# When the second weight tile and x rows 4 to 7 are loaded, and where three small steps of the up stage stand

## The chip, the cores and the metric

The kernel runs on one core of one Trainium2 chip. The core has five engines with instruction streams of their own: TensorE (PE: matmuls, and transposes as matmuls against an identity), VectorE (DVE), ScalarE (ACT), GpSimd (POOL) and SyncE (SP, which here only starts DMAs). They meet only at semaphores. The metric is the device time of one execution in microseconds (us), as the median of several runs.

## The reference, cut to what matters

One decoder layer on x of 1024 tokens by 1024 channels, float32:

```
p = x @ w_in                    # all mixer projections, 128 columns per weight tile
y = four attention branches on p, gated by sigmoid(x @ w_gate + b_gate), summed, @ w_out
x = layer_norm(2**0.25 * x + y)
a = x @ w_up                    # 1024 -> 2816; a = causal conv of width 3 over tokens
h = gelu(a) * (x @ w_ffn_gate)
out = layer_norm(2**0.25 * x + h @ w_down)
```

The change touches the very start (x and the first two weight tiles of w_in) and the beginning of the up stage (x @ w_up, x @ w_ffn_gate, conv, gelu).

## The kernel before

**High and low parts.** A float32 matrix is split into a rounded high part and the rest, the low part, and a product is three matmuls (hi·hi, hi·lo, lo·hi). ACT writes every high part, DVE or POOL subtracts it to make the low part. So an operand is ready only after two engines have worked one behind the other.

**The opening (step "x").** x has eight rows of 128 tokens, 512 KB each. ACT's queue starts the loads of rows 0 to 3 and then of the second weight tile (number 1, 512 KB in pieces of 512 bytes). SP's queue starts weight tile 0 (in two DMAs, of 96 and of 32 columns, the second with pieces of 128 bytes) and right behind it, waiting for nothing, rows 4 to 7. PE turns (transposes) each row in two halves, so there are 16 halves n = 0 to 15. For each half ACT writes the high part into act_hi (line 1354), then DVE the low part into act_lo (line 2142). After half 7 PE waits for all eight low parts and starts the first projection (line 737) over the tokens of rows 0 to 3. Its 24 matmuls come in four parts of six; in front of the third and the fourth stands half 8, half 9. In front of the fifth part, the first of the second projection, stands half 10. That fifth part waits for the high and the low part of weight tile 1 together (`weights`, `low=True`). Further parts follow, with the halves up to 15 among them, and then a wait for all 16 low parts.

ACT also makes the high part of the weight tiles (line 1326, `split_weights`), at fixed places of its stream: tile 0 behind half 5, tile 1 behind half 7. POOL makes the low part (line 1751) once the high part is there. Behind half 3 ACT starts two small DMAs (forget bias, sinks).

**The up stage.** Each block of 128 hidden columns (n = 0 to 21) needs seven products of half-size matrices (a Strassen-like scheme), named p = 1 to 7. The table PRODUCTS sets their order: (0,1) (1,1) (0,2) (1,2), then (0,6) (0,5) (0,7) (0,3) (0,4), (1,6) (1,5) (1,7) (1,3) (1,4), and from n = 2 (n,1) (n,6) (n,2) (n,5) (n,7) (n,3) (n,4). Products 6, 5, 7, 3 use weight sums which DVE makes in `weight_sums` (w_sum, line 2184). ACT copies the operand (op_hi, line 1371), POOL subtracts (op_lo, line 1761), PE multiplies (line 1092, twelve matmuls), and DVE adds what PE left to other products (`combine`, line 2184: up_s, gate_s). PE waits for such a sum before (n,7) (the sum of (n,6)), before (n,3) (the sum of (n,5)) and before (n,4) (the sum of (n,7)), because the product is accumulated on a bank that the sum reads. `weight_sums(q + 7)` stands behind every combine, so the sums run seven products ahead. The sums of the tokens' parts have low parts too, called t_lo 13 to 16 for the last of four token groups, on POOL (line 1833); product (0,6) needs 13, (0,5) 14, (0,7) 15 and (0,4) 16. Behind (n,4) DVE adds two taps of the convolution (line 2513). `operand_sums` are the sums for the later down stage (dn_sums), two of them behind (1,5) and two behind (1,7).

Of the kernel before, what the change touches and what calls it, by code (L numbers as in the profile page):

```python
# [254 lines left out]
AT = {np_: q for q, np_ in enumerate(PRODUCTS)}  # L255
OP_SLOTS = 8
OP_EARLY = 4
OP_AHEAD = 6
# [31 lines left out]
def build_layer(nc, x, w_in, b_forget, sinks, w_branch, w_gate, b_gate, w_out, ln1_g, ln1_b,  # L290
                w_up, w_ffn_gate, conv_w, conv_b, w_down, ln2_g, ln2_b, out):
    STEPS = steps()
# [8 lines left out]
    with ctx:  # L301
# [4 lines left out]
        w_raw = sb("w_raw", [P, 2, 1024])  # L306
# [82 lines left out]
        x_loaded = [sem(f"x_loaded{t}") for t in range(NTOK)]  # L389
# [5 lines left out]
        raw_loaded = [sem(f"raw_loaded{k}") for k in range(2)]  # L395
# [152 lines left out]
        def ring_sources(step):  # L548


            kind = step[0]
            win = w_in[0]
            if kind == "iq":
                return [(w_tile(win, IQ + P * step[1], P), NKT, P, None)]
            if kind == "ik_f_iw":

                return [((w_tile(win, IK, 96), w_tile(win, IN_WIDTH - 32, 32)), NKT, P, None)]
            if kind == "kv_c":
                return [(w_tile(win, CK, P), NKT, P, None)]
            if kind in ("q", "k", "v"):  # L560
                col = {"q": Q_COL, "k": K_COL, "v": V_COL}[kind][step[1]]
                return [(w_tile(win, col + P * step[2], P), NKT, P, None)]
            if kind == "attn" and step[2] < PAIRS - 1:
                br, pr = step[1], step[2] + 1
                return [src for k in (("k", "q", "v") if br in (B, D) else ("q",)) for src in ring_sources((k, br, pr))]
            if kind == "merge":
                br, res = step[1], []
                for dt in range(NKT + 1):
                    if dt < NKT:
                        res.append((w_tile(w_gate[0], br * D_MODEL + dt * P, P), NKT, P, None))  # L570
                    if br == FINAL and 4 <= dt < NKT:
                        res.append(wo_source(dt - 4))
                    if dt >= 1:
                        res.append((w_tile(w_branch[0, br], (dt - 1) * P, P, 4), 4, P, None))
                return res
            if kind == "outproj":
                return [wo_source(k) for k in range(4, NKT)]
            return []

        def ring_view(buf, g, kt, cols):  # L580
            return buf[:, g % 2, 0:kt * cols].rearrange("p (k c) -> p k c", c=cols)
# [550 lines left out]
        def _(sp):  # L1132
            ring = Tally()
# [73 lines left out]
                sp.dma_start(h_slot(n), src).then_inc(h_loaded[n % H_SLOTS], 16)  # L1207

            load_weights(ring_sources(STEPS[1])[0])
            ring.next()  # L1210
            for t in range(4, NTOK):
                sp.dma_start(mid[:, t, :], x[0, t * P:(t + 1) * P, :]).then_inc(x_loaded[t], 16)

            def forget_bias(h):
# [7 lines left out]
            for step in STEPS[3:]:  # L1222
# [57 lines left out]
                if step[0] == "down":  # L1280
                    for n in range(NDOWN):
# [7 lines left out]
                        if n in ROWS_AT:  # L1289
                            t = ROWS_AT.index(n)  # L1290
# [20 lines left out]
        def _(act):  # L1311
            ring, chunks, obanks, pts, vparts = Tally(), Tally(), Tally(), Tally(), Tally()
# [204 lines left out]
            pt_released = released_chunks()  # L1517
            for t in range(4):
                act.dma_start(mid[:, t, :], x[0, t * P:(t + 1) * P, :]).then_inc(x_loaded[t], 16)
            dram, kt, cols, _k = ring_sources(STEPS[2])[0]  # L1520
            act.dma_start(ring_view(w_raw, 1, kt, cols), dram).then_inc(raw_loaded[1], 16)
            for step in STEPS:
                kind = step[0]
                if kind == "x":
                    for n in range(2 * NTOK):
                        t, c = n // 2, n % 2
                        act.wait_ge(x_turned, n + 1)
                        part(act_hi[:, 4 * c:4 * c + 4, t * P:(t + 1) * P],
                             x_bank(n).rearrange("p (k t) -> p k t", k=4))
                        if n == 3:  # L1530
                            act.wait_ge(forget_set, 1)
                            act.dma_start(forget[F_AT:P, :], b_forget[0].rearrange("(h a) -> h a", a=1)
                                          ).then_inc(params_loaded, 16)
                            act.dma_start(sink[:, :], sinks[0].partition_broadcast(P)).then_inc(params_loaded, 16)
                        if n in (5, 7):
                            split_weights()
                elif kind == "iq":
                    src = pair_in(1 - step[1])
# [198 lines left out]
        def _(pool):  # L1737
# [65 lines left out]
            for step in STEPS:  # L1803
                needed += len(ring_sources(step))
                if step[0] == "attn":
                    br, pr = step[1], step[2]
                    if (br, pr) == (C, 0):
                        normalise(br, 0)
                    if pr == 0:
                        normalise(br, 1)  # L1810
                    for g in range(len(chunk_stream(br)) + 2):
                        for _p, u in asked(br, pr, g):
                            if u % 2 == 1:
                                normalise(br, u // 2)
                        if splits_at(br, pr, g):
                            split_weights()
                else:
                    split_weights(min(needed + (1 if step[0] == "v" else 2), len(ring_list)) - ring.n)
                    if step[0] == "v":
                        normalise(step[1], 0)  # L1820
                    if step[0] == "x":
                        pool.wait_ge(params_loaded, 32)
                        nc.gpsimd.tensor_scalar(sink_neg[:], sink[:], -1.0, None, ALU.mult).then_inc(consts_ready, 1)
                    if step == ("osplit", D):
                        pool.wait_ge(bias_used, 2 + HEADS)
                        distances().then_inc(dist_ready, 1)
                if step[0] == "outproj":
                    for j in range(4):
                        if j == 3:
                            operands(AT[0, 5])  # L1830
                        for i, p in enumerate((6, 5, 7, 4)):
                            pool.wait_ge(t_hi, 4 * j + i + 1)
                            nc.gpsimd.tensor_tensor(token_block(p, 1, j), t_source(p, 2 * j + 1),
                                                    token_block(p, 0, j).bitcast(F32), ALU.subtract).then_inc(t_lo, 1)
                        if j >= 1:
                            operands(2 * j - 1)
                if step[0] == "up":
                    for q in range(len(PRODUCTS)):
                        operands(q)
                if step[0] == "down":  # L1840
                    for n in range(NDOWN):
                        split_down(n)

        @block.vector
        def _(dve):
# [429 lines left out]
            for step in STEPS:  # L2275
# [193 lines left out]
                elif kind == "up":  # L2469
# [11 lines left out]
                    for q in range(4, len(PRODUCTS)):  # L2481
# [24 lines left out]
                        elif p == 4:  # L2506
# [9 lines left out]
                                if back == 1:  # L2516
                                    own(ins)
                            ins.then_inc(conv_done, 1)
                        weight_sums(q + OP_AHEAD + 1)
                        for _step in range(SUM_STEPS[min(max(n - 1, 0), 1) + (n == LAST)].get(p, 0) if n else 0):  # L2520
                            next(summing)
                    split_h(4)
# [106 lines left out]
```

## Time and profile before

| what | us |
|---|---|
| median of 3 runs | 2154.56 |
| lowest, highest | 2153.33, 2155.11 |
| the profiled execution | 2150.87 |
| its span in the trace | 2149.1 |
| PE busy | 2095.7 |
| DVE busy | 1482.3 |
| ACT busy | 935.0 |
| POOL busy | 802.3 |

The span is what the trace covers; the execution's own time is 1.8 us longer. A row of the timeline has the start, the duration, the engine, the line and operation, what is written from what, and in brackets how long the engine stood idle before and who released it. Several equal instructions in a row are merged (x2), and the duration is then that of the group.

### The profile page before, as it was taken

To read this page: it belongs to the slowest core of one execution; us is meant where nothing else is said; L and a number is where in the kernel's file an instruction comes from. 1 tells how busy PE (TensorE), PEld (TensorE's weight loads), DVE (VectorE), ACT (ScalarE), POOL (GpSimd) and SP (SyncE) were. 2 spreads that over 40 slices of the span, in tenths; PEclk is the share of its full clock that TensorE was granted. 3 is DMA by queue.
4 is the path that set the end of the run, shared out by engine and by line. 5 is a ranking of instruction groups with operands and counts; after the bars stand their busy time and mean duration, and the time that the engine had idled before them with its cause. 6 is when DMAs were issued, how large, how long until landed. Compare 5 with 4: busy or idle time off the path is not lost.

```text
span 2149.1 us, 28592 instructions
## 1 busy us (share of the span) xinstructions
PE 2095.7 (98%) x10468; PEld 1750.0 (81%) x10468; DVE 1482.3 (69%) x2532; ACT 935.0 (44%) x1671; POOL 802.3 (37%) x630
## 2 busy tenths in 40 slices
PE   8999999999999999999999999999999999999998
PEld 6788888788888888888877888888788888887887
DVE  4976767866788666666756772177877777775658
ACT  4565563126731265563126662232433333344541
POOL 2133332223322223332222332324765555555741
PEclk9999999999999999999999999999999999999999
DMA  3301101120012311112120002241566665558862
GB/s 128 41 21 30 30 16 35 45 54 21 15 45 80 87 40 30 40 45 74 45 63 2 16 11 74 79 147 50 157 190 202 182 191 176 160 193 303 276 199 94
DMA packets 198621, 198.05 MB, mean 92 GB/s; under 512 B 25161, under 2 KB 157257, under 8 KB 198481
## 3 DMA queue, kind: packets, MB, share of 16 engines
q1 hardware_dynamic: 194960, 187.26, 28.6%
q10 hardware_dynamic: 3520, 8.95, 1.2%
q8 instruction: 84, 1.38, 0.3%
q14 instruction: 57, 0.46, 0.1%
HBM read 151.06 MB, written 45.12 MB: 91 GB/s over the span
## 4 chain that ended last, share of the span: by engine, by line
PE 81%; DVE 12%; issue 3%; ACT 3%; POOL 1%; DMA 1%; DVEq 0%; SPq 0%; ACTq 0%
PE pair L737 25%; PE pair L1092 13%; PE pair L753 11%; PE obank L1092 5%; PE pair L1121 4%; PE obank L850 4%; PE chunk L829 4%; PE pair L1051 3%; DVE o_top L1899 3%; PE pair L801 3%; PE chunk L1121 2%; PE pair L802 2%; PE obank L1121 2%; DVE pt_lo L2071 1%; DVE heads L2142 1%
## 5 line engine op out<-in xcount | busy, mean ns | idle before, releaser
L1751 POOL TENSOR_TENSOR w_lo<-w_raw,w_hi 128x1024 fp32r<-128x1024 f32 (+1 forms) x102 | 219.0, 2147 | 547.6 <-ACT w_hi L1326 547.3
L737 PE MATMUL pair<-act_hi,w_hi 128*128 128x512 f32 x704 | 278.4, 396 | 4.1 <-DVE act_lo L2142 3.1
L737 PE MATMUL pair<-act_lo,w_hi 128*128 128x512 f32 x704 | 274.3, 390 | 0.0
L737 PE MATMUL pair<-act_hi,w_lo 128*128 128x512 f32 x704 | 272.4, 390 | 0.0
L1326 ACT ACTIVATE w_hi<-w_raw 128x1024 fp32r<-128x1024 f32 (+1 forms) x102 | 94.0, 922 | 366.8 <-PE pair L737 347.1
L2071 DVE TENSOR_TENSOR pt_lo<-chunk,pt_hi 128x512 fp32r<-128x512 f32 (+1 forms) x272 | 173.2, 639 | 71.5 <-ACT pt_hi L1354 66.9
L1354 ACT ACTIVATE pt_hi<-chunk 128x512 fp32r<-128x512 f32 (+1 forms) x272 | 150.7, 554 | 154.9 <-PE chunk L829 153.2
L1799 POOL TENSOR_SCALAR prob<-prob,att 128x256 f32<-128x256 f32 (+4 forms) x172 | 117.6, 694 | 255.0 <-DVE att L2015 255.0
L1899 DVE TENSOR_SCALAR_CACHE_REDUCE o_top<-score,stat 128x384 uint8<-128x384 f32 (+1 forms) x186 | 164.9, 943 | 14.0 <-issue 12.9
L753 PE MATMUL pair<-act_hi,w_hi 128*128 128x512 f32 x384 | 166.6, 434 | 0.4 <-DVE heads L2020 0.3
L737 PE MATMUL pair<-heads,w_hi 128*128 128x512 f32 x512 | 158.0, 390 | 1.7 <-DVE mid L2395 1.7
L737 PEld LDWEIGHTS pair<-act_hi,w_hi 128*128 128x128 f32 x704 | 132.3, 188 | 30.9 <-DVE act_lo L2142 3.8
L737 PEld LDWEIGHTS pair<-act_hi,w_lo 128*128 128x128 f32 x704 | 132.1, 188 | 27.9
L737 PEld LDWEIGHTS pair<-act_lo,w_hi 128*128 128x128 f32 x704 | 132.4, 188 | 24.9
L850 PE MATMUL obank<-pt_hi,heads 128*128 128x256 f32 (+1 forms) x568 | 150.8, 289 | 1.7 <-DVE o_t L2079 1.2
L753 PE MATMUL pair<-act_hi,w_lo 128*128 128x512 f32 x384 | 152.4, 397 | 0.0
L753 PE MATMUL pair<-act_lo,w_hi 128*128 128x512 f32 x384 | 151.9, 396 | 0.0
L1418 ACT ACTIVATE prob<-prob,att 128x256 f32<-128x256 f32 (+4 forms) x172 | 120.6, 702 | 43.7 <-DVE att L2003 42.0
L850 PE MATMUL obank<-pt_lo,heads 128*128 128x256 f32 (+1 forms) x568 | 139.5, 282 | 0.0
L801 PE MATMUL pair<-heads 128*128 128x512 f32 (+3 forms) x352 | 120.7, 349 | 11.8 <-DVE att L2003 6.1
L829 PE MATMUL chunk<-ident,prob 128*128 128x128 f32 x660 | 112.5, 275 | 4.6 <-DVE pt_lo L2071 3.1
L850 PEld LDWEIGHTS obank<-pt_hi,heads 128*128 128x128 f32 x568 | 108.2, 190 | 8.4 <-DVE o_t L2079 2.3
(345 smaller groups left out, 5091.1 us busy)
## 6 DMA issues: line engine op xcount, KB each, us to landing
down_sums<-dn_sums SPq DMA_DIRECT2D x40, 512.0 KB, 6.3
w_raw<-in_w_in SPq DMA_DIRECT2D x36, 512.0 KB, 3.8
w_raw<-in_w_gate SPq DMA_DIRECT2D x32, 512.0 KB, 4.0
up_raw<-in_w_up SPq DMA_DIRECT2D x22, 512.0 KB, 4.8
gate_raw<-in_w_ffn_gate SPq DMA_DIRECT2D x22, 512.0 KB, 6.0
hidden<-gelu_s SPq DMA_DIRECT2D x22, 512.0 KB, 3.3
dn_raw<-down_sums SPq DMA_DIRECT2D x44, 256.0 KB, 4.3
h_in<-down_sums SPq DMA_DIRECT2D x44, 256.0 KB, 4.7
```

The lines of the kernel that those rows point to most:

```text
L737: last = nc.tensor.matmul(dst[0:cols, s:s + HALF], w[:, k, :], a[:, k, s:s + HALF], start=(i == 0), stop=(i == len(order) - 1))
L753: last = nc.tensor.matmul(pair[1][:, s:s + HALF], w[:, k, :], a[:, k, s:s + HALF], start=(k == 0 and n == 0), stop=(k == NKT - 1 and n == 2))
L801: nc.tensor.matmul(dst[:, s:s + m], q, k_hi[:, s:s + m], start=True, stop=False)
L829: last = nc.tensor.transpose(t[:, at:at + P], prob_slot(br, 2 * j + w)[:, s:s + P], ident[:])
L850: last = nc.tensor.matmul(obank[BANK_OF[j] % 2][:, q0:q0 + width], v, part[:, slot, at:at + width], start=(c == 0 and b == 0 and w == 0), ...
L1092: last = nc.tensor.matmul(dst, w[:, cols], moving, start=(p in (1, 6, 5) and k == 0 and m == 0), stop=(k == 3 and m == 2), skip_group_chec ...
L1121: last = nc.tensor.matmul(banks[t], l[:, t * P:(t + 1) * P], r, start=(p in (6, 1, 5, 3) and k == 0 and m == 0), stop=(k == KFF - 1 and m ...
L1354: nc.scalar.activation(dst, src, func, **kw).then_inc(act_part, 1)
L1418: last = nc.scalar.activation(prob_slot(br, u)[:, 0:n], prob_slot(br, u)[:, 0:n], ACT.Exp, bias=att_stat(0, u), scale=-1.0, accum_out=att_ ...
L1751: nc.gpsimd.tensor_tensor(split_into(1, g), w_raw[:, g % 2, 0:kt * cols], split_into(0, g).bitcast(F32), ALU.subtract).then_inc(lo_ready, 1)
L1899: nc.vector.tensor_scalar(junk[:, b % 2, 0:(i + 1) * P], s, limit if isinstance(limit, float) else limit[:, b:b + 1], None, ALU.is_ge, ALU ...
L2071: nc.vector.tensor_tensor(pt_lo[:, n % PT_SLOTS, 0:m], t[:, 0:m], pt_hi[:, n % PT_SLOTS, 0:m].bitcast(F32), ALU.subtract).then_inc(chunk_f ...
```

## The change

It makes five moves and adds or removes no arithmetic.

1. The load of weight tile 1 goes from ACT's queue to SP's, between rows 5 and 6.
2. On SP, rows 4 and 5 wait until row 1 has landed; tile 1, rows 6 and 7 until row 3 has landed.
3. On ACT, the split of weight tile 1 goes from behind half 7 to behind half 9, and the two small DMAs from behind half 3 to behind half 13.
4. On POOL, the low part of the operand of (0,7) goes in front of t_lo 16.
5. On DVE, `weight_sums` is skipped behind (0,4), so that the first two sums of block 2 are made at the next call, behind the combine of (1,6).

```diff
             load_weights(ring_sources(STEPS[1])[0])
-            ring.next()
             for t in range(4, NTOK):
+                if t % 2 == 0:
+                    sp.wait_ge(x_loaded[t - 3], 16)
+                if t == 6:
+                    load_weights(ring_sources(STEPS[2])[0])
                 sp.dma_start(mid[:, t, :], x[0, t * P:(t + 1) * P, :]).then_inc(x_loaded[t], 16)
...
             for t in range(4):
                 act.dma_start(mid[:, t, :], x[0, t * P:(t + 1) * P, :]).then_inc(x_loaded[t], 16)
-            dram, kt, cols, _k = ring_sources(STEPS[2])[0]
-            act.dma_start(ring_view(w_raw, 1, kt, cols), dram).then_inc(raw_loaded[1], 16)
...
-                        if n == 3:
+                        if n == 13:
                             act.wait_ge(forget_set, 1)
...
-                        if n in (5, 7):
+                        if n in (5, 9):
                             split_weights()
...
                         for i, p in enumerate((6, 5, 7, 4)):
+                            if (j, p) == (3, 4):
+                                operands(AT[0, 7])
                             pool.wait_ge(t_hi, 4 * j + i + 1)
...
                             ins.then_inc(conv_done, 1)
-                        weight_sums(q + OP_AHEAD + 1)
+                        if (n, p) != (0, 4):
+                            weight_sums(q + OP_AHEAD + 1)
```

On ACT, the start of the program before (act_hi is written from the PSUM banks chunk and obank, two halves of a row each; w_hi is the high part of a weight tile):

```order
L1519 DMA mid<-in_x 128x1024 x4
L1521 DMA w_raw<-in_w_in 128x8x128
L1354 ACT_TABLE_LOAD
L1354 ACTIVATE act_hi<-chunk 128x4x128 x2
L1354 ACTIVATE act_hi<-obank 128x4x128 x2
L1532 DMA forget<-in_b_forget 8x1
L1534 DMA sink<-in_sinks 128x8
L1354 ACTIVATE act_hi<-chunk 128x4x128 x2
L1326 ACTIVATE w_hi<-w_raw 128x1024
L1354 ACTIVATE act_hi<-obank 128x4x128 x2
L1326 ACTIVATE w_hi<-w_raw 128x1024
L1354 ACTIVATE act_hi<-chunk 128x4x128 x2
```

And of the changed kernel, whose line numbers are higher by three:

```order
L1522 DMA mid<-in_x 128x1024 x4
L1357 ACT_TABLE_LOAD
L1357 ACTIVATE act_hi<-chunk 128x4x128 x2
L1357 ACTIVATE act_hi<-obank 128x4x128 x2
L1357 ACTIVATE act_hi<-chunk 128x4x128 x2
L1329 ACTIVATE w_hi<-w_raw 128x1024
L1357 ACTIVATE act_hi<-obank 128x4x128 x2
L1357 ACTIVATE act_hi<-chunk 128x4x128 x2
L1329 ACTIVATE w_hi<-w_raw 128x1024
L1357 ACTIVATE act_hi<-obank 128x4x128 x2
L1357 ACTIVATE act_hi<-chunk 128x4x128 x2
L1533 DMA forget<-in_b_forget 8x1
```

The second w_hi now stands behind halves 8 and 9, the small DMAs left the place behind half 3, and one DMA left the queue. PE's own order is the same in both kernels.

On POOL, where the up stage begins, before (t_ and act_lo are the low parts t_lo 13 to 16, op_late and op_early the operands' low parts):

```order
L1761 TENSOR_TENSOR op_late<-w_sum,op_late 128x512 x2
L1833 TENSOR_TENSOR t_49<-mid,t_49 128x512
L1833 TENSOR_TENSOR act_lo<-mid,act_hi 128x4x128
L1833 TENSOR_TENSOR t_49<-t_sum,t_49 128x512
L1833 TENSOR_TENSOR t_51<-t_sum,t_51 128x4x128
L1761 TENSOR_TENSOR op_late<-w_sum,op_late 128x512 x2
L1761 TENSOR_TENSOR op_early<-gate_raw,op_early 128x512
```

Of the changed kernel one of the last two op_late, that of (0,7), stands a place higher, and t_51 (t_lo 16) behind it:

```order
L1836 TENSOR_TENSOR t_49<-t_sum,t_49 128x512
L1762 TENSOR_TENSOR op_late<-w_sum,op_late 128x512
L1836 TENSOR_TENSOR t_51<-t_sum,t_51 128x4x128
L1762 TENSOR_TENSOR op_late<-w_sum,op_late 128x512
L1762 TENSOR_TENSOR op_early<-gate_raw,op_early 128x512
```

On DVE, from the combine of (0,4) on, before:

```order
L2184 SCALAR_TENSOR_TENSOR gate_s<-first_s,pair 128x512
L2513 SCALAR_TENSOR_TENSOR conv_s<-up_s,convw,conv_s 128x1023
L2513 SCALAR_TENSOR_TENSOR conv_s<-up_s,convw,conv_s 128x1022
L2184 SCALAR_TENSOR_TENSOR w_sum<-gate_raw 128x512
L2184 SCALAR_TENSOR_TENSOR w_sum<-w_sum,up_raw 128x512
L2184 SCALAR_TENSOR_TENSOR up_s<-first_s,pair 128x512
L2184 SCALAR_TENSOR_TENSOR gelu_s<-gelu_s,gate_s 128x1024
L2184 SCALAR_TENSOR_TENSOR gate_s<-first_s,obank 128x512
```

Of the changed kernel the combine of (1,6), which writes up_s, comes in front of the two w_sum; the rows from gelu_s on are at their old places:

```order
L2516 SCALAR_TENSOR_TENSOR conv_s<-up_s,convw,conv_s 128x1023
L2516 SCALAR_TENSOR_TENSOR conv_s<-up_s,convw,conv_s 128x1022
L2187 SCALAR_TENSOR_TENSOR up_s<-first_s,pair 128x512
L2187 SCALAR_TENSOR_TENSOR w_sum<-gate_raw 128x512
L2187 SCALAR_TENSOR_TENSOR w_sum<-w_sum,up_raw 128x512
L2187 SCALAR_TENSOR_TENSOR gelu_s<-gelu_s,gate_s 128x1024
```

## Rows read from the trace of the kernel before

**Rows 1.** The page: busy time of PE, and the chain that ended last.

```profile
PE 2095.7 (98%) x10468; PEld 1750.0 (81%) x10468; DVE 1482.3 (69%) x2532; ACT 935.0 (44%) x1671; POOL 802.3 (37%) x630
...
PE 81%; DVE 12%; issue 3%; ACT 3%; POOL 1%; DMA 1%; DVEq 0%; SPq 0%; ACTq 0%
```

**Rows 2.** Windows: engines' busy time and instructions, clock, DMA share, GB/s.

```profile
1550.00:1900.00 350.00, 350.00 (x1546) 289.82 (x1545) 262.73 (x295) 133.56 (x203) 207.45 (x130) 1.00 0.61 184
```

**Rows 3.** Timeline of PE and its weight loads, the opening: start, us, instruction, idle before.

```profile
5.24 1.94 PE L942 MATMUL chunk<-ident,mid 128*128 128x128 f32 x8 [5.24 <-DMA mid<-in_x]
...
7.29 1.57 PEld L942 LDWEIGHTS obank<-ident,mid 128*128 128x128 f32 x8 [0.51 <-DMA mid<-in_x]
...
9.06 1.18 PE L942 MATMUL chunk<-ident,mid 128*128 128x128 f32 x8
...
14.25 0.50 PE L737 MATMUL pair<-act_hi,w_hi 128*128 128x512 f32 x1 [2.85 <-DVE act_lo L2142]
...
21.15 0.48 PE L737 MATMUL pair<-act_hi,w_hi 128*128 128x512 f32 x1
```

**Rows 4.** Timeline of ACT, the opening.

```profile
9.30 0.60 ACT L1354 ACTIVATE act_hi<-obank 128x512 fp32r<-128x512 f32 x1 [0.26 <-PE obank L942]
...
9.88 0.36 ACTq L1534 DMA_DIRECT2D sink<-in_sinks  x1
10.29 1.08 ACT L1354 ACTIVATE act_hi<-chunk 128x512 fp32r<-128x512 f32 x2 [0.39 <-PE chunk L942]
11.26 1.06 ACT L1326 ACTIVATE w_hi<-w_raw 128x1024 fp32r<-128x1024 f32 x1
12.21 1.09 ACT L1354 ACTIVATE act_hi<-obank 128x512 fp32r<-128x512 f32 x2
17.27 1.06 ACT L1326 ACTIVATE w_hi<-w_raw 128x1024 fp32r<-128x1024 f32 x1 [3.98 <-DMA w_raw<-in_w_in]
...
19.59 0.60 ACT L1354 ACTIVATE act_hi<-chunk 128x512 fp32r<-128x512 f32 x1 [0.78 <-PE chunk L942]
```

**Rows 5.** Timeline of POOL, the opening.

```profile
18.41 2.40 POOL L1751 TENSOR_TENSOR w_lo<-w_raw,w_hi 128x1024 fp32r<-128x1024 f32 x1 [3.58 <-ACT w_hi L1326]
```

**Rows 6.** DMAs: tile 0's second issue; the x rows' times to landing.

```profile
w_raw<-in_w_in SPq DMA_DIRECT2D x1, 128.0 KB, 9.9
...
DMA to landing us min/median/max: 4.4/9.2/12.6
```

**Rows 7.** DMA queues from 7 to 8 us: packets, MB, share of 16 engines.

```profile
q10 hardware_dynamic: 107, 0.40, 97.0%
q1 hardware_dynamic: 106, 0.01, 8.6%
```

**Rows 8.** Timeline of POOL, the up stage's start.

```profile
1517.94 3.00 POOL L1833 TENSOR_TENSOR t<-t_sum,t 128x512 fp32r<-128x512 f32 x2
1520.90 3.44 POOL L1761 TENSOR_TENSOR op_late<-w_sum,op_late 128x512 fp32r<-128x512 f32 x2
```

**Rows 9.** Timeline of DVE, the up stage's start.

```profile
1524.82 0.67 DVE L2184 SCALAR_TENSOR_TENSOR gate_s<-first_s,obank 128x512 f32<-128x512 f32 x1
...
1535.99 0.68 DVE L2184 SCALAR_TENSOR_TENSOR w_sum<-gate_raw 128x512 f32<-128x512 f32 x1
...
1537.32 0.68 DVE L2184 SCALAR_TENSOR_TENSOR up_s<-first_s,pair 128x512 f32<-128x512 f32 x1
...
1542.45 0.68 DVE L2184 SCALAR_TENSOR_TENSOR gate_s<-gate_s,pair 128x512 f32<-128x512 f32 x1
```

**Rows 10.** Timeline of PE, products (0,7), start of (0,3), (1,7), (1,4).

```profile
1522.78 2.97 PE L1092 MATMUL pair<-t,op_late 128*128 128x512 f32 x12 [0.72 <-POOL op_late L1761]
1525.59 0.47 PE L1092 MATMUL obank<-act_hi,op_late 128*128 128x512 f32 x1
...
1538.05 3.01 PE L1092 MATMUL pair<-t,op_early 128*128 128x512 f32 x12 [1.29 <-DVE up_s L2184]
...
1543.62 2.88 PE L1092 MATMUL pair<-t,op_late 128*128 128x512 f32 x12
```

## The prediction, put down before the changed kernel ran

> **What bounds the kernel now.** I read the page first. PE is busy 2095.7 of 2149.1 us, and the chain that ended last lies on PE for 81% [rows 1]. So an edit counts only where PE waits, and a microsecond won or lost there is handed on by everything behind it. The windows say how far it is handed on: from 1550 to 1900 us PE is busy 350.00 of 350.00 us [rows 2], without a gap that could swallow a shift. Then I read the timelines of the two places that the change touches, each engine by itself. In the opening the reader is to see PE idle for 2.85 us until 14.25, released by DVE, and to follow that wait back through ACT [rows 3, 4]. In the up stage two waits of PE are left: 0.72 us before product (0,7), released by POOL, and 1.29 us before (1,7), released by the DVE sum up_s [rows 10]. What the change may win is near these 4.9 us; what it may lose is a new wait.
>
> **Opening, the earlier start of PE.** ACT does half 3 from 9.30 to 9.90, but halves 4 and 5 begin only at 10.29, right behind the second small DMA, whose issue ends at 9.88 + 0.36 = 10.24 [rows 4]. PE turns halves 4 and 5 from 9.06 to 10.24, eight transposes in one group, so half 4 is there at about 9.65 and half 5 at 10.24 [rows 3]. With the two issues gone, half 4 runs beside the transposes of half 5. Half 5 starts at 10.28 instead of 10.77 (10.29 and half of the 0.97 us to the split at 11.26), and the split of tile 0 at about 10.77 instead of 11.26. Halves 6 and 7 follow (before at 12.21), then DVE, then PE. That is 0.49 us, if tile 0 is there. Its second DMA took 9.9 us to land [rows 6]; issued at about 1.2 us this is 11.1 us. From 7 to 8 us ACT's queue (q10) and SP's (q1) moved 107 and 106 packets, of which SP's carried only 0.01 MB [rows 7]: the two queues take turns by the packet, so the small pieces of tile 0 wait for the large ones of rows 0 to 3. These are the same after the change. What is gone is tile 1 behind them on ACT's queue, so tile 0's tail gets the engines to itself at the end. The bounds are 0 (it lands as late as before) and 0.5; I take 0.4 won, near the upper one, since the last pieces lose their partner.
>
> The Trainium skill bears on this ("DMA: Bandwidth & Descriptors", section "Queues, rings and completion order"): each engine consumes a queue's descriptors in ring order and goes round between the queues. By that rule holding back rows 4 to 7, which stood behind tile 0 on its own ring, cannot hasten tile 0 at all; the equal packet counts agree with the taking of turns. If nothing else hastened it, the 0.4 would be 0 and the sum below 0.4 higher.
>
> **Opening, the later low part of tile 1.** This is the largest term, and it is a loss. PE's fifth part starts at 21.15, 6.90 us behind the first matmul at 14.25 [rows 3], and it waits for tile 1's low part. Before, the split began at 17.27, when the tile landed, took 1.06, and POOL's low part ran from 18.41 to 20.81 [rows 4, 5]. That was 0.34 us ahead of need. Now the split stands behind half 9. ACT does half 9 at 19.59, released by PE [rows 4], and a following copy starts about 0.49 later (the step of the pair at 10.29), so at 20.08. It ends at 21.14, POOL starts 0.08 later (as 18.33 to 18.41) and ends at 21.22 + 2.40 = 23.62. PE starts at about 23.66 instead of 21.15: 2.5 us lost. Both times hang on PE's start, so the 0.4 moves them alike and the 2.5 stays. What could shorten it? Half 9's copy cannot be earlier, since PE turns it behind the third part. That tile 1 lands earlier wins nothing, since ACT does not look at it before. The bounds are 2.2 (a shorter step on ACT and POOL) and 2.8 (a POOL operation of 2.6 and slower hand-overs); I take 2.5, from the rows.
>
> The split no longer blocks half 8, which frees nothing: no PE wait lies between 14.25 and 21.15. The small DMAs behind half 13 take 0.94 us of ACT's stream (9.30 to 10.24) ahead of half 14, which is 1.8 us behind half 13 as half 11 is behind half 10, so they are hidden; if they were not, up to 0.4. Their data is first needed some 10 us later. On SP, rows 4 and 5 start at 7.3, when row 1 lands [rows 3]. Row 4 is needed when half 8 is turned, 2.8 us behind PE's start, at about 16.7. All of rows 0 to 3 and tile 0 is 2.6 MB, so at the 0.41 MB per us of [rows 7] the engines are free at about 10, and row 4, 0.5 MB, lands at 12 to 13. Cost 0.
>
> **Up stage, the low part in front of t_lo 16.** POOL makes t_lo 15 and 16 from 1517.94 to 1520.94, 1.5 us each, and then the low parts of (0,7) and (0,3) from 1520.90 to 1524.34, 1.7 each [rows 8]. With the new order (0,7)'s is ready at about 1521.2 and not 1522.65, so PE could start (0,7) at 1522.06, where its 0.72 us of idleness began. But the next product, (0,3), waits for the DVE sum of (0,5), which runs from 1524.82 to 1525.49, and (0,3) started at 1525.59, already at its heels [rows 9, 10]. That sum stands behind others on DVE that did not wait for the moved step. So PE runs (0,7) earlier and then stands still before (0,3). Also (0,3)'s own low part is still made second, at 1524.3. I take 0; the bounds are 0 and 0.72. t_lo 16 is now ready at 1522.7 and needed by (0,4) at about 1528.4; nothing is lost.
>
> **Up stage, the two sums.** The combine of (1,6) stood behind two sums at 1535.99 and began at 1537.32 [rows 9]; PE's (1,7) started at 1538.05, 0.05 after its end. Now the combine runs from 1535.99 to 1536.67, and (1,7) starts at 1536.76, where its idleness began: 1.29 won at this point. The two sums then fill 1536.6 to 1538.0, so from the next instruction on DVE is where it was. And DVE has no gap there: its combine of (1,7) still ends at 1542.45 + 0.68 = 1543.13, and PE's (1,4), which needs it, cannot start before 1543.17. It started at 1543.62 [rows 9, 10]. So 0.45 remains of the 1.29. The bounds are 0 and 1.29; I take 0.45. The low parts of block 2 come 0.6 us later and are needed more than ten us later, so they are covered.
>
> **The sum.** -0.4 + 2.5 + 0 - 0.45 = +1.65 us. Against the profiled execution's own 2150.87 that makes 2152.5. The median of the runs is 2154.56, 3.7 above the profiled one, so on the scale of the medians the forecast is 2156.2.
>
> **Rivals.**
>
> *The new wait does not appear (faster).* If PE met tile 1's low part in time, the opening would win 0.4 to 0.5, and the up stage 0.45 to 1.29 and perhaps 0.72 more. With the best of each: -2.5, which is 2152.1. For it speaks that the change brings tile 1 in sooner; against it that the low part is chained to half 9 on ACT by order, with 3.5 us of work behind it and only 1.6 us until PE asks (19.59 to 21.15).
>
> *The rows come late (slower).* Rows 4 to 7 are now asked for 5 us later and upon arrivals. The longest landing of a row was 12.6 us [rows 6]. If row 4, asked for at 7.3, needed as much, it would come at 19.9, and PE would stand 3.2 us before half 8, ahead of everything else: 1.65 + 3.2 = +4.9, 2159.4. It decides from a landing time of 9.4 us on. Against it: the 12.6 came with five transfers of 0.5 MB in the queues, and now there is little ahead.
>
> *PE falls to the slower clock in the new gap (slower, but small).* The first eight transposes took 1.94 us and a later eight 1.18 [rows 3], at a granted clock of 1.00 in both; if the 2.5 us of idleness brought such a slow stretch back for twice eight steps, that would cost 2 x 0.76 = 1.5: +3.2, 2157.7. Against it: after 2.85 us of idleness the matmul at 14.25 took 0.50 and the one at 21.15, with no gap, 0.48 [rows 3].
>
> The Trainium skill ("TensorE: Matmul & The Clock Gate", section "What's actually happening") says that the array's clock falls to 1.2 GHz when PE has been idle; the trace shows no such fall behind its own gap of 2.85 us, which is longer than the new one.
>
> **Chances.** Forecast, with the 0.4 and 0.45 anywhere in their bounds: 0.75. No new wait: 0.07. Rows late: 0.08. Slow clock: 0.05. The rest, 0.05, for what I don't see. A measurement of this kernel can tell about 0.2%, 4.3 us, from no change. The forecast, the faster rival and the slow clock all lie within it; only late rows go beyond. With the spread of medians (1.8 us between the runs shown) I say faster 0.03, within 0.2% 0.88, slower 0.09. The range: below, 2153.4, where the terms fall to their better ends (-0.5 + 2.2 - 1.29 = +0.4, with 1.6 for the spread); above, 2159.0, which takes in the slow clock and most of the late rows.
>
> **What would show it.** Right: PE idle about 2.5 us before the fifth part, released by POOL's w_lo; its first matmul at about 13.85; the second w_hi right behind half 9's copy; no wait on x rows; up_s of (1,6) in front of the w_sum pair; the wait before (1,7) gone and short ones before (0,3), (1,3) or (1,4), released by DVE. Wrong: a fifth part that starts without a wait, a wait on a DMA of x between 16 and 27 us, a first matmul still at 14.25, or (0,7)'s 0.72 won for good.

## The result, and the profile after

| | before | changed |
|---|---|---|
| median of 22 runs each, us | 2153.47 | 2156.48 |
| lowest, highest | 2152.15, 2155.16 | 2153.58, 2158.90 |
| the profiled execution | 2150.87 | 2156.33 |
| its span | 2149.1 | 2154.5 |

The ratio is 1.0013, with a 95% interval of 1.0007 to 1.0019. So the changed kernel is slower, by 3.0 us (0.14%). That is less than the 0.2% which the prediction took as what can be told from no change. The forecast was 2156.2. It was made on a base of three runs with a median of 2154.56. The base of 22 runs lies 1.1 lower, so the forecast sum of +1.65 must be held against 3.0.

The page of the changed kernel, the line that answers to the first of [rows 1]:

```profile
PE 2099.4 (97%) x10468; PEld 1752.0 (81%) x10468; DVE 1481.8 (69%) x2532; ACT 934.9 (43%) x1671; POOL 802.3 (37%) x630
```

PE has 3.7 us more of busy time with the same 10468 instructions. No instruction was added, so some of them took longer. The timeline of PE in the opening (start, duration, instruction, and in brackets the idle time and its releaser) answers to [rows 3]:

```profile
13.78 0.50 PE L737 MATMUL pair<-act_hi,w_hi 128*128 128x512 f32 x1 [2.35 <-DVE act_lo L2145]
...
23.25 0.77 PE L737 MATMUL pair<-act_hi,w_hi 128*128 128x512 f32 x1 [2.31 <-POOL w_lo L1752]
23.81 0.63 PE L737 MATMUL pair<-act_lo,w_hi 128*128 128x512 f32 x1
```

The first matmul starts 0.47 earlier (14.25 to 13.78). The fifth part starts at 23.25 instead of 21.15, behind a wait for POOL's w_lo. Its matmuls take 0.77 and 0.63, where before they took 0.48 and less. ACT's timeline, against [rows 4], shows where that wait was made:

```profile
9.82 1.08 ACT L1357 ACTIVATE act_hi<-chunk 128x512 fp32r<-128x512 f32 x2
10.77 1.07 ACT L1329 ACTIVATE w_hi<-w_raw 128x1024 fp32r<-128x1024 f32 x1
...
19.14 0.60 ACT L1357 ACTIVATE act_hi<-chunk 128x512 fp32r<-128x512 f32 x1 [1.23 <-PE chunk L942]
19.63 1.05 ACT L1329 ACTIVATE w_hi<-w_raw 128x1024 fp32r<-128x1024 f32 x1
...
30.85 0.60 ACT L1357 ACTIVATE act_hi<-obank 128x512 fp32r<-128x512 f32 x1 [1.23 <-PE obank L942]
```

The split of tile 1 stands right behind half 9, for which ACT had stood idle 1.23 us. POOL follows (compare [rows 5]):

```profile
20.76 2.34 POOL L1752 TENSOR_TENSOR w_lo<-w_raw,w_hi 128x1024 fp32r<-128x1024 f32 x1 [6.40 <-ACT w_hi L1329]
```

Windows of PE over the same place (window, its length, PE's busy time and instructions, granted clock, DMA share, GB/s):

```profile
22.00:23.00 1.00, 0.00 (x0) 0.94 0.00 0
23.00:24.00 1.00, 0.75 (x2) 0.50 0.00 0
...
25.00:26.00 1.00, 1.00 (x4) 0.50 1.15 342
26.00:27.00 1.00, 1.00 (x10) 0.85 0.24 62
27.00:28.00 1.00, 1.00 (x7) 1.00 0.05 12
```

Towards the end of the 2.31 us in which PE did nothing, the granted clock fell to 0.50, the lower of its two levels (1.2 GHz), and it came back after some 3.4 us, most of them busy. The next common landmark behind it is the wait for all 16 low parts. It ends at 32.90; before, the same matmul stood at 29.38, so the shift is now 3.52. Of these, 2.10 were there at 23.25 and 1.42 came with the slow clock.

The up stage, PE, against [rows 10]:

```profile
1525.40 2.88 PE L1092 MATMUL pair<-t,op_late 128*128 128x512 f32 x12
1529.10 0.47 PE L1092 MATMUL obank<-act_hi,op_late 128*128 128x512 f32 x1 [0.81 <-issue]
...
1540.40 3.02 PE L1092 MATMUL pair<-t,op_early 128*128 128x512 f32 x12
1543.58 0.50 PE L1092 MATMUL obank<-act_hi,op_late 128*128 128x512 f32 x1 [0.17 <-DVE gate_s L2187]
...
1546.85 1.45 PE L1092 MATMUL pair<-t,op_late 128*128 128x512 f32 x5 [0.26 <-DVE gate_s L2187]
```

And DVE beside it, against [rows 9]:

```profile
1528.32 0.68 DVE L2187 SCALAR_TENSOR_TENSOR gate_s<-first_s,obank 128x512 f32<-128x512 f32 x1
...
1539.65 0.69 DVE L2187 SCALAR_TENSOR_TENSOR up_s<-first_s,pair 128x512 f32<-128x512 f32 x1
...
1546.12 0.68 DVE L2187 SCALAR_TENSOR_TENSOR gate_s<-gate_s,pair 128x512 f32<-128x512 f32 x1
```

(0,7) starts without a wait, but (0,3) then waits 0.81. The row names no releaser ("issue"), but the wait ends 0.10 behind the end of DVE's gate_s at 1529.00. From (0,3) to (1,4) it was 1543.62 - 1525.59 = 18.03; now it is 1546.85 - 1529.10 = 17.75. So 0.28 is won. The runs of single parts below agree: 17.77 in up_only (1527.77 to 1545.54), 18.02 in opening_only (1528.80 to 1546.82).

That leaves a shift of 3.23 at (1,4), and yet the spans differ by 5.4. Most of the missing 2.2 lies in the down stage, which the change doesn't touch. Before, PE's timeline there reads:

```profile
1951.97 2.90 PE L1121 MATMUL pair<-dn_last,h_more 128*128 128x512 f32 x6 [2.90 <-issue]
1954.66 1.67 PE L1121 MATMUL chunk<-dn_last,h_more 128*128 128x512 f32 x6
1956.17 1.52 PE L1121 MATMUL pair<-dn_last,h_more 128*128 128x512 f32 x6
```

In the changed kernel:

```profile
1955.62 2.90 PE L1121 MATMUL pair<-dn_last,h_more 128*128 128x512 f32 x6 [3.15 <-issue]
1958.31 2.76 PE L1121 MATMUL chunk<-dn_last,h_more 128*128 128x512 f32 x6
1960.87 1.91 PE L1121 MATMUL pair<-dn_last,h_more 128*128 128x512 f32 x6
```

At full clock a group of six takes 1.52. Behind the same gap, one group ran slow before and two and a part ran slow after: another 1.4 us. Of the rest, 0.4 had come up before this stretch (0.25 of it in the longer gap) and 0.3 came behind it; they were not followed up. Whether that belongs to the change is a question for the experiments.

### The profile page after: what moved, and what is told of

It is laid out like the page before. It is cut to its first block, busy times and chain, and to the rows that moved or that the text cites. A ratio compares the mean times of both kernels' runs of the same rounds, so it can differ in the third digit from the quotient of the medians.

```text
span 2154.5 us, 28592 instructions
## 1 busy us (share of the span) xinstructions
PE 2099.4 (97%) x10468; PEld 1752.0 (81%) x10468; DVE 1481.8 (69%) x2532; ACT 934.9 (43%) x1671; POOL 802.3 (37%) x630
## 4 chain that ended last, share of the span: by engine, by line
PE 81%; DVE 12%; issue 3%; ACT 3%; POOL 1%; DMA 1%; DVEq 0%; SPq 0%; ACTq 0%
PE pair L737 25%; PE pair L1092 13%; PE pair L753 11%; PE obank L1092 5%; PE pair L1121 4%; PE obank L850 4%; PE chunk L829 4%; PE pair L1051 3%; DVE o_top L1902 3%; PE pair L801 3%; PE chunk L1121 2%; PE pair L802 2%; PE obank L1121 2%; DVE pt_lo L2074 1%; DVE heads L2145 1%
```

## The experiments

### Each half alone, and the split back at its place

Theory: all of the loss is the late low part of tile 1. Rivals: the up stage loses too, or the loads do.

`opening_only` undoes the two edits of the up stage, `up_only` undoes all three of the opening. `split_at_7` is the changed kernel with

```diff
-                        if n in (5, 9):
+                        if n in (5, 7):
```

> The changed opening on the up stage of before. Order theory: all of the change's loss lies here. First matmul at about 13.78, half 9's copy at 19.14, tile 1's low part done at 23.1, PE released at 23.25 with a matmul step of about 0.43 us until 26, and everything from there about 3.5 us later than before; the time 2.5 to 4 us above before. Rival, up-stage theory: the changed up stage carries the loss, and this kernel is within 1 us of before.

> The opening of before, with the two changed steps of the up stage. My theory: the earlier low part of (0,7) buys nothing, because (0,3) then waits for the DVE sum of (0,5); the sums behind (1,6) buy 0.1 to 0.5 us. Product (0,7) starts without a wait at about 1521.9, (0,3) still at 1525.6, (1,4) at 1543.3, (2,1) at 1546.2; the time 0 to 0.5 us below before, not to be told from it. Rival: the steps win 1.29 + 0.72 = 2.0 us, and (2,1) starts at 1544.3.

> The changed kernel with tile 1's split put back behind half 7. Order theory: the wait before the fifth part and the slow stretch behind it both vanish; ACT waits for tile 1 at about 12.8 until it lands (14 to 17), the low part is ready before PE asks at 20.7, and the kernel is 3.5 to 4 us faster than the changed one and 0.5 us faster than before. Rival, load theory: tile 1, now between rows 5 and 6 and asked for at 10.1, lands later than 17.3, and PE waits before the fifth part here too.

Measured, against 33 runs of before on the same chip (2153.12):

| kernel | median us | ratio, 95% interval |
|---|---|---|
| opening_only | 2155.69 | 1.0013 (1.0004 to 1.0022) |
| up_only | 2152.96 | 1.0000 (0.9991 to 1.0009) |
| split_at_7 | 2152.29 | 0.9998 (0.9989 to 1.0006) |

PE in the opening of opening_only has the wait and the slow clock again:

```profile
23.14 0.77 PE L737 MATMUL pair<-act_hi,w_hi 128*128 128x512 f32 x1 [2.31 <-POOL w_lo L1752]
```

In split_at_7, ACT's second split follows the landing of tile 1:

```profile
10.88 1.06 ACT L1329 ACTIVATE w_hi<-w_raw 128x1024 fp32r<-128x1024 f32 x1
14.79 1.06 ACT L1329 ACTIVATE w_hi<-w_raw 128x1024 fp32r<-128x1024 f32 x1 [1.88 <-DMA w_raw<-in_w_in]
```

Tile 1 was there at 14.79 instead of 17.27, although it was asked for 7 us later. POOL was done at 18.31, PE's fifth part started at 20.79 without a wait, and the x stage ended at 29.02 (before 29.38, changed 32.90). One number, 9 for 7, holds the whole loss. In the timeline the moved loads by themselves cost nothing.

### The two parts of the earlier start

The prediction gave 0.4 to the small DMAs' new place and argued that tile 0's landing stood close behind. `small_dmas_13` is the kernel before with only n == 13 for n == 3; `loads_only` has only the new loads, with both splits at their old places.

> The kernel before with only the two small DMAs moved from behind half 3 to behind half 13. Issue theory: they alone held halves 4 and 5, so half 4's copy comes right behind half 3's at 9.8 and the first matmul 0.45 us earlier against row 0's transposes. Rival, load theory: tile 0 still lands at 11.1 behind tile 1's pieces, its split starts no earlier than 11.1, and the first matmul comes at most 0.2 us earlier.

> The kernel before with only the loads changed: rows 4 to 7 upon arrivals and tile 1 between rows 5 and 6. Issue theory: the first matmul stays where it was, 9.0 us behind the start of row 0's transposes, and only tile 1 lands earlier (14.8 and not 17.3). Rival, load theory: the first matmul comes about 0.5 us earlier.

Each ran once, for its profile. ACT in small_dmas_13:

```profile
11.31 1.06 ACT L1326 ACTIVATE w_hi<-w_raw 128x1024 fp32r<-128x1024 f32 x1 [0.40 <-DMA w_raw<-in_w_in]
```

ACT was ready 0.40 earlier and then waited for tile 0: the first matmul stands at 14.29, as before. In loads_only tile 0 could have come sooner, but ACT was behind its small DMAs, and the split stands at 11.55. Both edits together bring it to 10.77 (10.88 in split_at_7). So the 0.5 is a joint gain. For the loads alone that is in part argued: in loads_only PE's eight transposes of halves 4 and 5 also took 1.91 us, against 1.18 before, which by itself delays the split; that ACT would have been late anyway is read from its halves 4 and 5, which began at 10.33, behind the DMAs' end at 10.28. Nor do both edits bring the gain every time. `down_filled`, further down, has both, but its eight transposes took 1.72, its split stands at 11.41 and its first matmul at 14.39. These transposes come back below.

### The clock in the new gap

Theory: 1.4 of the 3.5 us are the slow clock behind PE's 2.31 us of idleness, and it falls for want of work. `gap_filled` is the changed kernel with 14 transposes of the identity in that gap, their result used by nobody:

```diff
+                        if n == 4:
+                            for _ in range(14):
+                                nc.tensor.transpose(pair[1][:, HALF:HALF + P], ident[:], ident[:])
                         next(first[n // 4])
```

> The changed kernel with 14 transposes of the identity, into a bank that is not in use yet, in the gap before the fifth part. Clock theory: PE is still released at about 23.2 by tile 1's low part, but its clock stays at 1.00 and the matmul step at 0.23, so everything behind is 1.2 to 1.3 us earlier than in the changed kernel. Rival, without the clock: the slow step is the waking of PE's pipe or a slow weight read, and it stays at 0.43; the time is then that of the changed kernel.

It took 2154.14, ratio 1.0008 (0.9999 to 1.0017). PE's timeline:

```profile
20.76 1.69 PE L957 MATMUL pair<-ident 128*128 128x128 f32 x14
23.25 0.47 PE L737 MATMUL pair<-act_hi,w_hi 128*128 128x512 f32 x1 [0.79 <-POOL w_lo L1755]
23.55 0.40 PE L737 MATMUL pair<-act_lo,w_hi 128*128 128x512 f32 x1
...
31.48 0.50 PE L737 MATMUL pair<-act_hi,w_hi 128*128 128x512 f32 x1 [0.25 <-DVE act_lo L2148]
```

The wait ends at 23.25, to the hundredth where it ended without the transposes. But the matmuls behind it take 0.47 and 0.40, and the x stage ends at 31.48 instead of 32.90. The clock's price was 1.42 in this pair of profiles. The medians on the same chip, 2155.69 for opening_only and 2154.14 here, point the same way, but with spreads of 6.6 and 5.0 us over eleven runs each they don't settle it.

### What holds back the up stage

Theory, from the prediction's fourth step: moving sums helps only if the combine that PE waits for next moves too. In the changed kernel (0,3) waits for the combine of (0,5), which stands behind the sums of (1,7) on DVE. `gate_sum_first` is split_at_7 with these sums made one call later:

```diff
                             combine(n, p, up_s[:, HALF:SEQ], first, place)
-                            weight_sums(q + OP_AHEAD + 1)
+                            weight_sums(q + OP_AHEAD + 1 - (n == 0))
...
-                        if (n, p) != (0, 4):
+                        if (n, p) not in ((0, 6), (0, 4)):
                             weight_sums(q + OP_AHEAD + 1)
```

> As split_at_7 (the changed kernel, tile 1 split behind half 7), but on DVE the combine of (0,5) comes in front of the sum w_sum for (1,7) and not behind it. My theory: the low part of (0,7) that the change makes earlier bought nothing because that combine held (0,3); now (0,3) starts right behind (0,7), without the 0.76 us of idleness, and (1,4) comes 0.7 us earlier against the start of (0,7). Rival: POOL's low part for (0,3) holds it all the same, and at most 0.2 us is won.

It took 2152.18, ratio 0.9996 (0.9987 to 1.0005), against 2153.0 for before. DVE:

```profile
1522.37 0.68 DVE L2187 SCALAR_TENSOR_TENSOR gate_s<-first_s,obank 128x512 f32<-128x512 f32 x1
1522.96 1.19 DVE L2187 SCALAR_TENSOR_TENSOR w_sum<-up_raw,gate_raw 128x512 f32<-128x512 f32 x1
```

PE:

```profile
1538.43 0.50 PE L1092 MATMUL obank<-act_hi,op_late 128*128 128x512 f32 x1 [0.45 <-DVE gate_s L2187]
...
1541.70 3.01 PE L1092 MATMUL pair<-t,op_late 128*128 128x512 f32 x12 [0.26 <-DVE gate_s L2187]
```

gate_s now stands in front of a sum of 1.19, and (0,3) started at 1523.88 without a wait. From (0,7) to (1,4) it is 1541.70 - 1521.15 = 20.55, against 21.40 in split_at_7 (1522.98 to 1544.38). So 0.85 was won, where the change by itself won 0.28. The timeline shows that; the total time, with an interval of 1.8 us in width, can't.

### The down stage's gap, and the spread between runs

Theory: the slow stretch of the down stage has no fixed length, and its changes are part of the spread between runs. `down_filled` is split_at_7 with 18 transposes of the identity in the gap:

```diff
                                 n = at_product * KFF + k
+                                if (n, t) == (8, 0):
+                                    for _ in range(18):
+                                        nc.tensor.transpose(pair[0][:, 0:P], ident[:], ident[:])
```

> As split_at_7, with 18 transposes of the identity into an unused bank in PE's gap of about 3 us in the down stage (near 1950 us). Clock theory: PE is released at the same time, its clock stays at 1.00 there in every run, the six matmuls behind the gap take 1.6 us and not 2.9, and the runs lie 0 to 2.8 us lower than those of split_at_7, with a smaller spread. Rival: the spread of the runs comes from elsewhere and stays at 4 us.

It took 2151.41 (2149.33 to 2152.36), ratio 0.9993 (0.9984 to 1.0002). PE:

```profile
1950.00 2.13 PE L1115 MATMUL pair<-ident 128*128 128x128 f32 x18
1953.39 1.61 PE L1124 MATMUL pair<-dn_last,h_more 128*128 128x512 f32 x6 [1.26 <-issue]
1954.84 1.52 PE L1124 MATMUL chunk<-dn_last,h_more 128*128 128x512 f32 x6
```

There is no slow group left, and the spread of eleven runs is 3.0 us, against 4.1 in gate_sum_first on the same chip and 4.4 in split_at_7 on another. Without the transposes the first three groups took 2.90, 1.67, 1.52 (before), 2.90, 2.76, 1.91 (changed), 2.90, 2.76, 1.92 (small_dmas_13) and 1.63, 1.52, 1.52 (split_at_7): in kernels with the same down stage the stretch was anything from none to two groups and a part. Of the nine profiles with this gap empty eight have a slow stretch, which makes the way from the first to the fourth group 1.4 to 2.8 us longer than the 4.18 of split_at_7; of the three with the gap filled none has. small_dmas_13, without the late split and its wait, has the long stretch too, so nothing here ties the extra 1.4 of the profiled pair to the change.

Two last kernels carry this to the opening's old gap. `before_filled` is the kernel before with the 18 transposes and 14 more in front of its first matmul; `all_filled` adds everything that had won (the new loads, the split at 7, gate_sum_first's order). Their second edit:

```diff
+                    for _ in range(14):
+                        nc.tensor.transpose(pair[1][:, HALF:HALF + P], ident[:], ident[:])
                     first = [project_parts(k, act_hi, act_lo, low_last=k == 0) for k in range(2)]
```

> The kernel before with 14 transposes of the identity in PE's gap ahead of the first matmul and 18 in its gap in the down stage; their results are used by nobody. Theory (slow stretches of the clock behind these two gaps make part of the run-to-run spread): the profile shows no matmul step of 0.43 us behind either gap, the fastest run stays near before's (2150.9) or 0.3 above it, and the median falls by 1 to 2 us, to about 2151.5 to 2152.5, with a smaller spread between runs. Rival (the clock in these gaps plays no part in the spread): median 2153 to 2154 and the spread of before. If the first eight transposes of the opening are still slow when the added ones begin, these take 3.4 and not 1.7 us and the opening loses about 1 us in such a run.

> Everything that the runs so far pointed to in one kernel: the second weight tile asked for late as in the changed kernel, but split behind half 7 as before; (0,5)'s combine ahead of the two sums; the transposes of the identity in both gaps. If the gains add (opening 0.4, up stage 1.1, the slow stretches of the clock 1 to 2): median 2150 to 2151, against 2153.3 for the kernel before in the same rounds, ratio about 0.9987. If only the order of work counts and the filled gaps give nothing: 2152, the median of gate_sum_first. In the up stage (0,7) to (1,4) stays 20.55 us.

| kernel | median us | lowest, highest | ratio, 95% interval |
|---|---|---|---|
| before, same chip, 21 runs | 2153.80 | 2150.51, 2155.51 | |
| before_filled, 11 runs | 2149.72 | 2148.68, 2151.84 | 0.9983 (0.9974 to 0.9992) |
| all_filled, 11 runs | 2148.58 | 2148.23, 2150.81 | 0.9976 (0.9967 to 0.9985) |

Adding 32 useless transposes to the kernel before makes it 4.1 us faster (1.7 to 5.6 by the interval), twice what was expected or more. PE in before_filled:

```profile
10.96 1.69 PE L949 MATMUL pair<-ident 128*128 128x128 f32 x14
14.24 0.50 PE L737 MATMUL pair<-act_hi,w_hi 128*128 128x512 f32 x1 [1.59 <-DVE act_lo L2147]
...
1951.36 1.63 PE L1126 MATMUL pair<-dn_last,h_more 128*128 128x512 f32 x6 [1.13 <-issue]
```

The first matmul is where it was (14.25), so nothing was won there in this pair. Behind the down stage's gap 1.4 was won. Another 1.0 was won in the attention, at a place where nothing had been filled (last section), and 0.4 of that was gone again before the down stage. But before's opening gap doesn't always leave the clock alone. up_only has before's opening unchanged, and in its profile the fall is there (windows of PE):

```profile
12.00:14.00 2.00, 0.13 (x2) 1.00 1.05 392
14.00:15.00 1.00, 0.53 (x2) 0.93 1.04 389
15.00:17.00 2.00, 2.00 (x6) 0.50 1.03 328
```

Its x stage ended at 31.17 instead of 29.38, 1.8 later, 0.2 of it before the first matmul. The same stretch stands in the profiles of down_filled (30.88) and loads_only (31.21), and not in the seven others that leave this gap empty.

These three have one more thing in common, and it comes before the gap: PE's transposes of halves 4 and 5. The first row is up_only's, the second down_filled's.

```profile
9.04 1.92 PE L942 MATMUL chunk<-ident,mid 128*128 128x128 f32 x8
9.16 1.72 PE L942 MATMUL chunk<-ident,mid 128*128 128x128 f32 x8
```

These eight took 1.92, 1.72 and 1.91 us where the clock fell later, and 1.04 to 1.18 in the seven profiles where it didn't. They took 1.04 in before_filled and in all_filled too. So these two profiles don't show that the transposes hold the clock in the opening's gap, since without them no fall was to be expected either; that is shown for the new gap by one profile, and for the down stage's gap by three.

Nor do the two filled gaps account for all of the 4.1. By the profiles with empty gaps, I estimate 1.8 on average for the down stage (nine profiles) and 0.5 for the opening (three falls in ten, at some 1.5 each behind the first matmul), 2.3 together. That lies within the interval; where more than that comes from stays open.

The order of work adds less than the filled gaps: all_filled lies 1.1 below before_filled, and its (0,7) to (1,4) is 20.52 us, as expected.

## Why the prediction was right, and where it wasn't

Sums below are of the profiled pair unless they say medians.

**The earlier start.** Forecast -0.4, measured -0.47. ACT's halves 4 and 5 at 9.82 and the split at 10.77 are the forecast's own figures. The question that it left open, whether tile 0's tail would land in time, was rightly seen as the one that decides: with the old loads it lands at 11.3 and the gain is 0. The reason given, that its last pieces lose tile 1 as their partner, wasn't tested apart from the holding back of rows 4 to 7. The first matmul also depends on how long the transposes before it run slow, which the forecast took as fixed (down_filled: 14.39).

**The low part of tile 1.** Forecast +2.5. Measured: a fifth part that could have started 6.90 behind the first matmul, at 20.68, started at 23.25, so +2.57. The chain was half 9 at 19.14, w_hi at 19.63, w_lo from 20.76 to 23.10, as worked out, but for a POOL operation of 2.34 instead of 2.40 and a start of PE 0.15 behind its end instead of 0.04. This step carried the forecast, and split_at_7 shows that it hangs on the place of the split alone.

**Rows and small DMAs.** Forecast 0 and hidden. No wait on x appears behind 13.78, and half 14 at 30.85 stands 1.82 behind half 13, as it would have without the two DMAs.

**The low part of (0,7).** Forecast 0, by the argument that (0,3) already stood at DVE's heels. That is what the trace shows: 0.72 gone before (0,7), 0.81 new before (0,3).

**The two sums.** Forecast -0.45, measured -0.28. The place was right: DVE's combine of (1,7) still starts 17.80 behind that of (0,5) (1546.12 - 1528.32), against 17.63 before [rows 9]. I had taken DVE's chain as fixed, and it grew by 0.17: behind the two taps of the convolution the first w_sum had started 4.03 after the taps' start (1535.99 - 1531.96), while up_s, now in its place, starts 4.19 after it (1539.65 - 1535.46). The kernel's code has the likely reason: the combine of (1,6) waits for the semaphore of the second tap (`conv_done`), and the first w_sum doesn't. In the five profiles where w_sum follows the taps it starts 0.07 to 0.08 before their end, in the seven where up_s follows it starts 0.09 to 0.11 behind it. The wait itself was not taken out in any run. The 0.17 is what is missing.

**The slow clock.** Here the prediction's argument failed, and it is the larger error. It was a rival with a chance of 0.05, priced at 1.5; it happened, at 1.42, on top of the forecast's own wait. The step that failed is the argument against it: one gap of 2.85 us without a fall was read as a rule ("the trace shows no such fall"). Of the ten profiles with this gap empty (2.3 to 2.9 us long) three show the fall, and it stands behind 2.31 us in both profiles that have the new one empty. So the length of the gap alone doesn't decide.

The section of the Trainium skill that was named there ("TensorE: Matmul & The Clock Gate", "What's actually happening") says that the throttled state is the default and activity lifts it. It also says that the number of slow matmuls at the start of a kernel differs between runs of one kernel. The opening agrees with the first: in each of the twelve profiles the first eight transposes took 1.94 us and later ones less, though the profile gives a granted clock of 1.00 for both. For the second there is only one profile of each kernel, but over the twelve kernels the transposes of halves 4 and 5 took between 1.04 and 1.92. One trace without a fall was not enough to rule a fall out.

**The sum.** -0.47 + 2.57 + 1.42 - 0.28 = +3.24, against 3.0 between the medians. The forecast of +1.65 was 1.4 short, which is the clock, and the base that was 1.1 too high hid most of that. So the time came out within 0.3 us partly by luck. The measured 2156.48 lies inside the stated range.

## What to carry to other kernels

An edit that moves a producer behind a consumer-driven step costs the whole chain behind that step (here split, low part and start of PE: 3.5 us of work against a slack of 1.6), whatever its input's arrival gains. A wait that is taken from one instruction is kept only if the next instruction's releaser moves too; look for it before counting the gain. A gap of TensorE of one to three us can be dearer than it looks: price the slower clock behind it, read it in several profiles rather than in one, and try idle transposes in it. Here they made the kernel before 4.1 us faster, of which some 2.3 are put down to the two gaps by the estimate above, and all reorderings together gave 1.1 more.

## What the runs showed of the hardware that I had not expected

**The spread between runs goes with the clock.** Each run has its mean granted clock. Of the 75 runs of before beside the experiments, the 23 at 0.993 took 2154.5 us on average, the 17 at 0.994 2153.4 and the 34 at 0.995 2152.4. Of split_at_7 the runs at 0.993, 0.994 and 0.995 took 2154.5, 2152.5 and 2150.8. Within one value the runs of before still lie up to 3.2 us apart (2150.56 to 2153.80 at 0.995), so the rounded clock explains a good half of the spread and not all of it.

**More such stretches.** PE in before, windows of 10 us (the last two figures are DMA share and GB/s):

```profile
510.00:520.00 10.00, 8.41 (x45) 0.83 0.19 54
540.00:550.00 10.00, 9.35 (x41) 0.66 0.01 2
570.00:580.00 10.00, 9.64 (x57) 1.00 0.01 2
```

and in all_filled:

```profile
510.00:520.00 10.00, 8.31 (x40) 0.70 0.16 48
...
570.00:580.00 10.00, 10.00 (x45) 0.72 0.00 2
```

The fall at 514 us in before stands right behind waits of PE in the attention of 1.21 and 0.39 us, shorter than any gap above. The profile of before_filled has the same two waits there, 1.23 and 0.39, at the same times to within 0.02 us, and no fall. Before:

```profile
514.30 0.43 PE L850 MATMUL obank<-pt_hi,heads 128*128 128x256 f32 x1 [0.39 <-DVE o_t L2079]
```

before_filled:

```profile
514.31 0.39 PE L850 MATMUL obank<-pt_hi,heads 128*128 128x256 f32 x1 [0.39 <-DVE o_t L2084]
```

At the next scores (line 801) before_filled is 1.04 us ahead, 517.06 against 518.10, with the same work. So a difference of 1 us between two profiles can be the clock alone. The stretches lie at one place in one kernel and at another in the next. Their gaps were not filled in any kernel here; what is left of the spread may be theirs, which was not tried.

**DVE's sums take longer beside POOL.** A pair of w_sum took 1.45 and 1.65 us from 1520.05 on, while POOL was busy, and the same two instructions, for block 2, 0.68 and 0.69 from 1535.99 on before [rows 9], where POOL had nothing to do. Others beside a busy POOL took between 1.18 (1525.41) and 1.79 (1523.11); a combine that reads a PSUM bank took 0.67 to 0.69 in both places. So such a pair in front of a combine costs 3.1 us in block 0 and only 1.3 in block 1. That POOL is the cause was not tested.
